# Attention in a two-layer diffusion trunk: the prompt's four units moved between the token tiles of the value projection, and two output chunks computed around the last unit's values

## The reference, cut to what matters

```python
qc, kc, vc = attn_project(hc, attn_wq[a], attn_wk[a], attn_wv[a])
yc = context_attention(qc, kc, vc, attn_sink[a]) @ attn_wo[a]
ql, kl, vl = attn_project(hl, attn_wq[a], attn_wk[a], attn_wv[a])
yl = latent_attention(axial_rope(ql), axial_rope(kl), vl,
                      cache_attn_k[:, a], cache_attn_v[:, a], attn_sink[a]) @ attn_wo[a]
new_k.append(kc)
new_v.append(vc)
...
xc = xc + mc[2] * yc
xl = xl + ml[2] * yl
```

## Time and profile before

| | |
|---|---|
| Median of three executions | 2055.31 us (2054.14 to 2056.89) |
| The profiled execution | 2054.8 us, its span 2053.0 us |
| Mean granted TensorE clock | 0.988 of full speed |
| PE busy | 1984.0 us (97% of the span) |
| DVE, ACT, POOL busy | 999.5, 663.4 and 777.3 us |

### The profile page before, as it was taken

How to read it: one execution, slowest core, us unless ns; L and a number is a source line. 1 busy time by engine, 2 the same in 40 slices (tenths; PEclk the granted TensorE clock), 3 DMA queues, 4 the chain that set the end, 5 groups by cost and what they waited for, 6 DMA issues and landing times.

```text
span 2053.0 us, 29532 instructions
## 1 busy us (share of the span) xinstructions
PE 1984.0 (97%) x11280; PEld 1695.6 (83%) x11280; DVE 999.5 (49%) x1333; ACT 663.4 (32%) x1323; POOL 777.3 (38%) x535
## 2 busy tenths in 40 slices
PE   6999999999999999999999999988989999999998
PEld 4787887888698768998998998885558998998996
DVE  3423430432343047662564476656625673675475
ACT  5332223213222315331332234325525331332232
POOL 4342333234333325333223334438835333333332
PEclk9999999999999999999999999999989999999999
DMA  8421332232133203432432222520003322222221
GB/s 341 164 72 62 124 113 92 93 113 72 62 125 112 77 36 114 154 113 72 154 130 94 74 72 82 172 78 1 1 21 115 122 82 82 73 72 82 72 72 52
DMA packets 53558, 195.75 MB, mean 95 GB/s; under 512 B 5968, under 2 KB 7376, under 8 KB 52432
## 3 DMA queue, kind: packets, MB, share of 16 engines
q1 hardware_dynamic: 48096, 174.68, 25.2%
q10 hardware_dynamic: 5360, 19.65, 2.5%
HBM read 187.23 MB, written 7.08 MB: 95 GB/s over the span
## 4 chain that ended last, share of the span: by engine, by line
PE 85%; DVE 4%; issue 3%; POOL 3%; ACT 2%; DMA 1%; DVEq 1%; SPq 1%; ACTq 1%; POOLq 0%
PE ps L440 35%; PE ps L483 21%; PE ps L455 17%; PE ps L653 2%; PE ps L683 2%; PE ps L502 2%; PE ps L393 1%; DVE front L1386 1%; ACT pr L1198 1%; POOL pr L1361 1%; DMA first_w<-first_dram 1%; POOL h_l L1285 1%; PE ps L397 1%; PE ps L838 1%; PE ps L530 1%
## 5 line engine op out<-in xcount | busy, mean ns | idle before, releaser
L1242 POOL TENSOR_TENSOR w_l<-raw,w_h 128x1024 fp32r<-128x1024 f32 x232 | 567.6, 2449 | 1057.4 <-ACT w_h L887 1057.4
L440 PE MATMUL ps<-h_h,w_h 128*128 128x384 f32 (+1 forms) x1696 | 529.3, 312 | 0.0
L440 PE MATMUL ps<-h_h,w_l 128*128 128x384 f32 (+1 forms) x1696 | 523.1, 308 | 0.0
L440 PE MATMUL ps<-h_l,w_h 128*128 128x384 f32 (+1 forms) x1696 | 523.0, 308 | 0.0
L887 ACT CAST w_h<-raw 128x1024 fp32r<-128x1024 f32 x232 | 245.3, 1059 | 554.6 <-PE ps L483 290.6
L440 PEld LDWEIGHTS ps<-h_h,w_h 128*128 128x128 f32 x1696 | 321.2, 189 | 12.6 <-issue 10.8
L440 PEld LDWEIGHTS ps<-h_l,w_h 128*128 128x128 f32 x1696 | 321.4, 189 | 2.5 <-issue 2.4
L440 PEld LDWEIGHTS ps<-h_h,w_l 128*128 128x128 f32 x1696 | 321.1, 189 | 0.0
L1643 DVE SCALAR_TENSOR_TENSOR cc<-ca,vec,cc 128x641 f32<-128x641 f32 x88 | 223.4, 2538 | 14.3 <-issue 13.1
L455 PE MATMUL ps<-w_h,h_h 128*128 128x512 f32 (+1 forms) x520 | 199.8, 384 | 1.0 <-issue 1.0
L455 PE MATMUL ps<-w_l,h_h 128*128 128x512 f32 (+1 forms) x520 | 198.2, 381 | 0.0
(11 more groups left out here) (202 smaller groups left out, 2809.6 us busy)
## 6 DMA issues: line engine op xcount, KB each, us to landing
raw<-stream_dram SPq DMA_DIRECT2D x312, 512.0 KB, 3.5
first_w<-first_dram SPq DMA_DIRECT2D x16, 512.0 KB, 15.7
gate<-gate_b_dram ACTq DMA_DIRECT2D x4, 1024.0 KB, 4.8
S<-state_dram ACTq DMA_DIRECT2D x4, 1024.0 KB, 7.2
new_state_dram<-st_out ACTq DMA_DIRECT2D x8, 512.0 KB, 3.8
xt<-x_dram ACTq DMA_DIRECT2D x5, 512.0 KB, 9.9
y_dram<-front SPq DMA_DIRECT2D x5, 512.0 KB, 2.6
rope_t<-rope_t_dram ACTq DMA_DIRECT2D x4, 512.0 KB, 3.6
```

The costliest lines, as they stand in the source:

```text
L440: mm = nc.tensor.matmul(ps[:, banks + half, 0:width(half)], w, x[:, k, lo_hi(half)], start=(k == 0 and n == 0), stop=(k == KT - 1 and n == 2))
L1242: nc.gpsimd.tensor_tensor(w_l[:, r, :], raw[:, s, :], w_h[:, r, :].bitcast(F32), ALU.subtract).then_inc(raw_used[s], 1)
```

## The change

The 20 units are computed in another order, the prompt's first. A table `PAIRS` now says which token block n and which half p each pair of units is. The prompt's four units are put between the five tiles of the value projection, which is now computed tile by tile with both weight chunks (`value_tile`) into banks 4 and 5. The transposes of the prompt's units all go to bank 6 (`turn_bank`). The transposes are split from the values (`unit_turns`).

At the end, `out_early` computes output chunks 0 and 1 for tiles 0 to 3 (24 matmuls of 512 columns each): chunk 0 ahead of the last unit's transposes, chunk 1 behind its values. `out_proj` then does only tile 4 of those chunks. Both halves of the output use banks 0 to 4, tile t in bank t, so the second half of tile t waits until the first half's residual of that tile is added.

On ACT, the stores of new keys and values move behind the exponentials of unit 6, the value tiles are copied out two at a time (`av_copy`), and the casts of output chunks 2 and 3 move behind the exponentials of the last unit. On POOL the matching two `lo` move behind the last unit.

The diff, cut to its core:

```diff
+PAIRS = ((4, 0), (4, 1), (0, 0), (0, 1), (1, 0), (1, 1), (2, 0), (2, 1), (3, 0), (3, 1))
+EARLY_PAIRS, EARLY_CHUNKS = 8, 2
...
+def turn_bank(x):
+
+    return 6 if x < KVH else 4 + x % 3
...
+            if early:
+                return t
             if mh == 0:
                 return (4 + t) % 8
             return (1, 2, 3, 0, 4)[t] if last else 1 + t
...
+                            if mh == 0 and chunks[0] < early and t < TT - 1:
+                                continue
...
+            def out_early(b, kc):
+
+                s = weights(b, kc, 0)
+                for t in range(TT - 1):
+                    for kk in range(2):
+                        k = 2 * kc + kk
+                        wh, wl = (w[:, s, kk * 512:(kk + 1) * 512] for w in (w_h, w_l))
+                        for n, (x, w) in enumerate(((h_h, wh), (h_h, wl), (h_l, wh))):
+                            nc.tensor.matmul(ps[:, t, :], x[:, k, t * P:(t + 1) * P], w,
+                                             start=(k == 0 and n == 0), stop=False)
...
-            for kc in range(2):
-                def free(t):
-                    if t == 4:
-                        pe.wait_ge(aqk_evac, 9)
-                token_chunk(b, 10 + kc, 0, kc, 4, KVH * HD, lambda t: (4 + t) % 8, free)
-            pe.wait_ge(aqk_evac, 10)
-            pe.wait_ge(av_evac, TT)
-            pe.wait_ge(arope_done, 10)
-            pe.wait_ge(at_in, 16 * AT_LOADS)
-            pe.wait_ge(at_bf, 1)
...
+            def value_tile(t):
+
+                bank, col = 4 + (t in (2, 3)), 256 * (t % 2)
+                if t == 4:
+                    pe.wait_ge(av_evac, 1)
+                for k in range(KT):
+                    at, s = slice(k % 4 * KVH * HD, (k % 4 + 1) * KVH * HD), slots[k // 4]
+                    for n, (x, w) in enumerate(((h_h, w_h), (h_h, w_l), (h_l, w_h))):
+                        mm = nc.tensor.matmul(ps[:, bank, col:col + 256], x[:, k, t * P:(t + 1) * P], w[:, s, at],
+                                              start=(k == 0 and n == 0), stop=(k == KT - 1 and n == 2))
+                if t < TT - 1:
+                    mm.then_inc(atile_done, 1)
+                else:
+                    mm.then_inc(chunk_done, 2)
+
+            value_tile(0)
+            pe.wait_ge(aqk_evac, 10)
             unit_scores(0)
-            for u in range(UNITS + 1):
+            value_tile(1)
+            unit_scores(1)
+            value_tile(2)
+            unit_turns(0)
+            unit_scores(2)
+            pe.wait_ge(av_evac, 1)
+            unit_values(0)
+            value_tile(3)
+            unit_turns(1)
+            unit_scores(3)
+            unit_values(1)
+            value_tile(4)
+            unit_turns(2)
+            pe.wait_ge(arope_done, 10)
+            pe.wait_ge(at_in, 16 * AT_LOADS)
+            pe.wait_ge(at_bf, 1)
+            unit_scores(4)
+            unit_values(2)
+            pe.wait_ge(av_evac, 3)
+            for u in range(KVH, UNITS + 1):
                 if u + 1 < UNITS:
                     unit_scores(u + 1)
-                if u >= 1:
-                    unit_values(u - 1)
+                if u == UNITS:
+                    pe.wait_ge(ae_done, 2 * UNITS)
+                    pe.wait_ge(aolo_done, EARLY_PAIRS)
+                    out_early(SEG["att_o"], 0)
+                unit_turns(u - 1)
+                unit_values(u - 1)
+            out_early(SEG["att_o"], 1)
             pe.wait_ge(aolo_done, UNITS // 2)
-            pe.wait_ge(ae_done, 2 * UNITS)
...
+            def free_att(mh, t):
+                if mh == 1:
+                    pe.wait_ge(res_done, 10 * 7 + t + 1)
...
+                if u in (UNITS, UNITS + 1):
+                    hi(b, u - UNITS + 10 + RING, 0)
...
+                if u in (0, 2, 3):
+                    av_copy((0, None, 1, 2)[u])
+                if u == 6:
+                    act.wait_ge(aqk_evac, 10)
+                    act.wait_ge(av_evac, 1)
+                    for kv in range(KVH):
+                        rows = slice(64 * (kv % 2), 64 * (kv % 2) + 64)
+                        act.dma_start(dr["new_k"][kv], ak[rows, kv // 2, 0:NCTX]).then_inc(kv_stored, 16)
+                    act.dma_start(dr["new_v"], av[:, 0, :]).then_inc(kv_stored, 16)
...
-                    for j in range(12):
+                    for j in range(10):
                         lo(SEG["att"], j + RING, 0)
...
+                    for j in (10, 11):
+                        lo(SEG["att"], j + RING, 0)
```

More of the change, by code:

```diff
@@ L141, with unit_keys @@
 PT_ACT = (1, 2)
-PT_AT = [sum(len(key_blocks(x // KVH)) for x in range(u)) for u in range(UNITS)]
-PT_OF = [kb in PT_ACT for u in range(UNITS) for kb in range(len(key_blocks(u // KVH)))]
+PAIRS = ((4, 0), (4, 1), (0, 0), (0, 1), (1, 0), (1, 1), (2, 0), (2, 1), (3, 0), (3, 1))
+EARLY_PAIRS, EARLY_CHUNKS = 8, 2
+def unit_keys(u):
+    return key_blocks(PAIRS[u // 2][0])
+PT_AT = [sum(len(unit_keys(x)) for x in range(u)) for u in range(UNITS)]
+PT_OF = [kb in PT_ACT for u in range(UNITS) for kb in range(len(unit_keys(u)))]
+def turn_bank(x):
+    return 6 if x < KVH else 4 + x % 3
 def over(ap, n):
@@ L335, in wait_lo, with out_bank @@
                     eng.wait_ge(done, len(mine) * n + need)
-        def out_bank(mh, t, last):
+        def out_bank(mh, t, last, early=0):
+            if early:
+                return t
             if mh == 0:
@@ L459, in token_chunk, with out_proj @@
                     elif last:
-                        mm.then_inc(tile_done if n_cols == 512 else atile_done, 1)
-            def out_proj(b, j0, i, tiles, xh, xl, ready, free, last=False, between=None):
+                        mm.then_inc(tile_done, 1)
+            def out_proj(b, j0, i, tiles, xh, xl, ready, free, last=False, between=None, early=0):
                 kcs = tiles // 2
@@ L474, in out_proj @@
                         for t in range(TT):
-                            bank = out_bank(mh, t, last)
+                            if mh == 0 and chunks[0] < early and t < TT - 1:
+                                continue
+                            bank = out_bank(mh, t, last, early)
                             if chunks[0] == 0:
@@ L860, in unit_values @@
                 mm.then_inc(apv_done, 1)
-            unit_scores(0)
-            for u in range(UNITS + 1):
+            slots = [weights(b, 10 + kc, 0) for kc in range(2)]
+            def value_tile(t):
[11 more added lines that the diff above has]
+                    mm.then_inc(chunk_done, 2)
@@ L873, in _ @@
+            out_early(SEG["att_o"], 1)
+            pe.wait_ge(aolo_done, UNITS // 2)
+            def free_att(mh, t):
+                if mh == 1:
+                    pe.wait_ge(res_done, 10 * 7 + t + 1)
+            out_proj(SEG["att_o"], 0, 0, KT, h_h, h_l, lambda kc: None, free_att, last=True,
+                     between=early_turns(3), early=EARLY_CHUNKS)
             ffn_phase(1, 8)
@@ L1175, in _ @@
                 hi(b, j + RING, 0)
-            hi(b, 10 + RING, 0)
-            for t in range(TT):
-                if t == TT - 1:
-                    act.wait_ge(chunk_done, b.done(11, 0))
-                else:
-                    act.wait_ge(atile_done, t + 1)
-                nc.scalar.copy(av[:, t, :], ps[:, (4 + t) % 8, 0:KVH * HD]).then_inc(av_evac, 1)
-            hi(b, 11 + RING, 0)
-            act.wait_ge(aqk_evac, 10)
-            act.wait_ge(av_evac, 1)
-            for kv in range(KVH):
-                rows = slice(64 * (kv % 2), 64 * (kv % 2) + 64)
-                act.dma_start(dr["new_k"][kv], ak[rows, kv // 2, 0:NCTX]).then_inc(kv_stored, 16)
-            act.dma_start(dr["new_v"], av[:, 0, :]).then_inc(kv_stored, 16)
             def unit_exp(u, half):
-                w, st = P * len(key_blocks(u // KVH)), stat[:, u % 3]
+                w, st = P * len(unit_keys(u)), stat[:, u % 3]
                 act.wait_ge(am_done, 2 * u + half + 1)
@@ L1217, in _ @@
                     o = (u - 3) // 2
-                    nc.scalar.copy(h_h[:, (o % 2) * G:(o % 2) * G + G, tok_of(o // 2)],
+                    n, p = PAIRS[o]
+                    nc.scalar.copy(h_h[:, p * G:p * G + G, tok_of(n)],
                                    ps[:, 7, :].rearrange("p (g q) -> p g q", g=G)).then_inc(aohi_done, 1)
@@ L1429, in residual_tile @@
                     dve.wait_ge(chunk_done, b.done(j0 + (mh + 1) * tiles // 2 - 1, i))
-                out, cols = ps[:, out_bank(mh, t, last), :], slice(mh * 512, mh * 512 + 512)
+                out, cols = ps[:, out_bank(mh, t, last, EARLY_CHUNKS if o == 7 else 0), :], slice(mh * 512, mh * 512 + 512)
                 V.tensor_tensor(out, out, gate[:, int(t == 0), cols], ALU.mult)
```

48 lines of the change are left out of this document (29 added, 19 removed).

## The result

The changed kernel takes 2038.97 us (median of 4 executions, 2037.32 to 2043.83) beside 2055.12 us for the kernel before on the same chip (4 executions, 2054.14 to 2056.89). The ratio is 0.9924, with a 95% interval of 0.9906 to 0.9943: 16.1 us less. The profiled execution took 2038.74 us, its span 2037.0 us, and the mean granted clock is 0.995 where it was 0.988. The forecast was 13.1 us less.

The account below looks back on a forecast made before the run. The loss was put at both ends of the units' stretch, where PE idles at a lowered clock. 23.3 - 7.2 - 1.0 - 2.0 = 13.1 us less gave 2042.2 us, own range 2038 to 2047, overall range 2037.5 to 2050.5.

Parts of the forecast that it names:

- The end: From the last units to the output's start: output starts as if at 1493.4 instead of 1516.7, a gain of 23.3 us.
- The front: Value tiles and prompt units: the first latent unit starts on POOL at 32.9 instead of 25.7, a loss of 7.2 us.
- handing over: Passing work between engines in the front, left out of the later steps: a loss of 1.0 us (0 to 2).
- prompt unit 3: Front step: same work as unit 2, with the first latent half ahead of its norm; starts on POOL at 28.2.
- copy 0.7: Front steps: a 512-wide copy ahead of a unit's values takes 0.7 us.
- The stores: ACT's 4.34 us of stores, moved between the latent units' exponentials and copies, partly covered: a loss of 2.0 us (0 to 4.3).
- The middle: The latent units keep their order on all engines: no cost either way, 7.36 us a unit.
- Costed at nothing: Includes moved casts and subtractions of output chunks 2 and 3 (8.9 us cover) and the output's residual waits: 0 us.
- The clock: 2.4 GHz assumed throughout; low level seen at PE busy 63 to 74%, new front 79%; a fall among value tiles refutes.
- Low clock in the front: Rival, chance 0.15: value matmuls behind the first gap run at low clock; gain falls by 5.3 to 7.8 us, 2047.5.
- No difference: Rival, chance 0.08: front and early chunks both at low clock, or the change misses its aim; 2051 to 2059 us.
- Slower: Rival, chance 0.08: the clock stays low into the latent units with four key blocks; 2067 us.

Follow-up runs that it names:

- order_only: The changed kernel without its two early output chunks, the output starting behind the last pair's remainder as before; 2043.96 us, ratio 0.9952.
- after_again: The changed kernel itself, unedited, run again as the reference of its set; 2040.38 us, ratio 0.9932 to the kernel before.
- stores_late: The changed kernel with the five stores of new keys and values behind the last unit instead of behind unit 6's exponentials; 2041.63 us, ratio 0.9938.
- values_first: The changed kernel with all five value tiles ahead of the prompt's first unit; 2049.26 us, ratio 0.9977.
- one_chunk: The changed kernel with only early chunk 0, ahead of the last unit's transposes, and none behind its values; 2042.83 us, ratio 0.9937.
- both_behind: The changed kernel with both early output chunks behind the last unit's values; 2043.37 us, ratio 0.9941.

## Why the prediction was right, and where it was not

**The end (23.3 us; measured 23.5): right.** L15 takes the place of the last prompt unit, and the output starts 5.2 us behind it; the forecast had 5.1 (1488.3 to 1493.4). order_only splits it: 19.4 us come from the order (28.7 to 9.3), 4.1 from the early chunks. The prediction worked out only the sum of the two.

**The front (7.2 us, with 1.0 for handing over: 8.2; measured 9.0 at L0): right to a microsecond.** The forecast starts on POOL were 9.4, 14.2, 20.6, 28.2 and 32.9; counted from K they are 9.5, 14.3, 20.9, 30.1 and 34.7. The step that was too short is prompt unit 3. Half of value tile 4 runs at the low clock there, and the tile takes 4.1 us and not 2.9. In after_again, order_only and stores_late, where the clock is at 1.00 through value tile 4 (in stores_late up to L0), unit 3 starts at K + 28.6 and L0 at K + 33.2, as the steps had it (28.2 and 32.9); the 1.0 us for handing over was then more than was needed. The rows of the changed kernel:

```profile
1373.77 0.65 PE L882 MATMUL ps<-pT,av 128*64 128x256 f32 x4 [1.77 <-DVE pT L1807]
...
1380.25 0.99 PE L882 MATMUL ps<-pT,av 128*64 128x256 f32 x4 [1.68 <-DVE pT L1807]
1381.17 0.58 PE L897 MATMUL ps<-w_h,h_h 128*128 128x256 f32 x1
...
1382.83 0.41 PE L897 MATMUL ps<-w_l,h_h 128*128 128x256 f32 x1
...
1384.00 0.28 PE L897 MATMUL ps<-w_l,h_h 128*128 128x256 f32 x1
```

The waits of 1.77 and 1.68 us before the values are not the "copy 0.7" of my steps alone. DVE's copy of unit 0's transposes stands behind the next unit's max and norm (the max starts at 1371.83, the copy runs from 1372.96 to 1373.62, the values start at 1373.77), so PE waits for all three, which the steps count as max, norm and copy; only 0.15 us of the 1.77 are handing over.

**The stores (2.0 us; measured 0): the term that was mis-sized.** The step was "Queued behind them are the copies for L1 and the exponentials of L3", priced between both bounds. The exponentials ahead of the stores had already been handed to the engine, so their issue (3.3 us in all, 1402.25 to 1405.54) ran under the exponentials' compute and under a wait for PE that was there anyway. stores_late shows the same: no gap goes away. On the common scale the gain is 14.7 us and not 13.1: these 2.0, 0.2 at the end and 0.2 between L0 and L15 more, less 0.8 in the front. The other 1.3 us between the traced spans (16.0) lie ahead of K and behind the output's start and are not explained by the change. That the total came so near is in part luck: a low clock in the front, which the sum had at nothing, cost 1.5 us, and what was put by for the stores (2.0) and for handing over (1.0) more than covered it.

**The middle (0): right.** 7.37 us from one unit to the next (1433.40 to 1440.77), before 7.36.

**Costed at nothing: right.** The two `lo` end on POOL at 1505.29. PE needs output chunk 2 at some 1514.5 (1511.82 and 12 matmuls), so the cover is 9.2 us (forecast 8.9). In the first 60 us of the output, to 1575, only two waits stand in the list of waits, 0.5 and 0.3 us, both behind the output in the ConvFFN: none for the residual.

**The clock.** The sum assumed full speed throughout. That held at the end (1.00) but not in front (0.93 in 1374.5 to 1400, 0.54 in value tile 4), and a fall among the value tiles was one of the prediction's own signs of being wrong. "Low clock in the front" was the rival with the most weight; it is seen in part, at 1.5 us at L0 (34.7 beside the 33.2 of stores_late, whose clock is at 1.00 up to there), not 5.3 to 7.8. The prediction's argument from PE's busy share (63 to 74% where the clock is low) is not borne out: order_only's window above has PE busy 23.42 of 32 us (73%) at 1.00. "No difference" is what values_first looks like: low clock in the front and at the early chunk, 3.7 us of gain left. "Slower" wanted a low clock that stays into the units with four key blocks; no trace here shows one in those units.

## What to carry to other kernels

Where a chain of small units ends a stage, put the narrow units where another wide piece of work can stand between them, and let the stage end with wide ones: this brought 10.6 of 14.7 us with no arithmetic changed, and with the early chunks but without the wide work between the narrow units only 3.7 were left (2.7 of the loss fell at the end, in a low clock whose cause is open). Then look on the bounding engine for each wait at the seam, and put there a piece of the next stage whose inputs are complete; a piece brings about the wait that it fills (2.4 to 2.9 us, 1.2 to 1.7 us), and not its own length (5.5 us). To price a block of DMA issues on a computing engine's queue, look at what that engine still computes and what it waits for behind them: 3.3 us of issue cost nothing here, where they stood behind exponentials still being computed and ahead of a wait for PE.

## What was not expected of the hardware

**The low clock in front has no fixed place.** Every trace of a kernel with the new front shows a stretch at the lower of the two levels (1.2 GHz) between value tile 1 and L2, but not at the same spot, even for the same program. In the changed kernel's trace it is 1381 to 1384, in value tile 4; in after_again tile 4 is at full clock, and the fall comes in L0 and L1:

```profile
1380.00:1386.00 6.00, 4.62 (x38) 4.06 (x40) 1.80 (x8) 2.57 (x11) 2.34 (x4) 1.00 0.00 0
1386.00:1392.00 6.00, 3.65 (x32) 1.86 (x30) 4.90 (x11) 2.56 (x9) 2.34 (x4) 0.93 0.00 0
1392.00:1398.00 6.00, 5.21 (x26) 2.77 (x26) 2.45 (x8) 2.53 (x10) 4.87 (x4) 0.50 0.00 1
```

One_chunk, whose front is word for word the same, is lowered three times: twice in the first of these windows (value tiles 1 to 3), once in the second:

```profile
1368.60:1380.60 12.00, 10.24 (x63) 9.35 (x62) 3.17 (x15) 3.42 (x18) 4.70 (x8) 0.72 0.00 1
...
1395.60:1401.60 6.00, 5.22 (x35) 3.05 (x34) 3.55 (x8) 2.80 (x10) 4.90 (x4) 0.72 0.01 1
```

PE's waits between the value tiles are the same in all these traces within 0.02 us (1.07 and 0.41 us at the first scores, 1.77 and 1.68 at the values). PE's share of busy time inside the low stretch is no guide either: it is busy 5.21 of 6 us at 0.50, in part because its matmuls take longer there. The price depends on the place. L0 at K + 33.2 (stores_late, clock at 1.00 up to there) and 19.3 us from L0 to L3 at 1.00 (changed kernel, 34.7 to 54.0) would put L3 at K + 52.5, an estimate from these traces. L3 stands at K + 54.0 in the changed kernel, 54.1 in after_again, 54.0 in order_only, and 53.1 in stores_late, with one stretch each, and at 55.5 in both_behind and one_chunk with two and three: 0.6 to 3.0 us. What sets the place stays open; no run here tells.

The Trainium skill ("TensorE: Matmul & The Clock Gate", A second HAM failure mode: psum-queue depth-cycling) describes a clock that goes back and forth in a kernel whose TensorE idles briefly and often between groups of matmuls. The traces agree that the clock falls and comes back in a stretch with waits of 0.4 to 1.8 us. Its price here is the 0.6 to 3.0 us estimated above, not the 5.3 to 7.8 that the prediction gave to it.

**A long low stretch.** In values_first the clock stays at 0.50 for all 18 us of the row above, with PE busy 12.94 of them, and the first prompt units follow each other by 5.6 us where they do so by 4.85 at full clock with a value tile between them (changed kernel, units 0 and 1). Narrow units with nothing wide between them waited and ran slowly at once here; whether the one keeps up the other is not shown.
